# A sixth weight slot, three projections moved into tile 1's recurrence, and V gathers traded against U gathers beside the recurrence

## What is computed

```python
mix = concatenate([att, hgrn_output(o, hg, hg_norm_gain)])
x = x + einsum('btm,md->btd', mix, w_out)                  # 1024 x 1024 weights
h2 = rms_norm(x, norm2_gain)
# peer_ffn, per token: 8 heads x 16 chosen experts = 128 rows of U and 128 rows of V
q = (h2 @ w_query).reshape(T, 8, 2, 128)                   # 1024 x 2048 weights
s = einsum('thcd,hcnd->thcn', q, sub_keys)
...                                                        # two top-16, then top-16 of the 256 sums: eidx, gate
act = gelu(einsum('thkd,td->thk', expert_u[eidx], h2))     # one dot per row of U
y = einsum('thk,thkd->td', gate * act, expert_v[eidx])     # weighted sum of rows of V
```

## Time and profile before

| | us |
|---|---|
| three runs, median (lowest to highest) | 2190.84 (2189.47 to 2190.89) |
| the profiled execution | 2188.74 |
| its span in the trace | 2186.6 |

### The profile page before, as it was taken

One profiled execution on the slowest core, in us unless ns is written; L12 is line 12 of the kernel. 1 busy time (PEld: TensorE's weight loads), 2 busy tenths in 40 slices (PEclk: granted clock), 3 DMA queues, 4 the chain that ended last, 5 costly groups with the idle time before them and its releaser, 6 DMA issues.

```text
span 2186.6 us, 15704 instructions
## 1 busy us (share of the span) xinstructions
PE 1222.7 (56%) x4932; PEld 548.7 (25%) x4932; DVE 1261.9 (58%) x2795; ACT 372.6 (17%) x1034; POOL 1166.5 (53%) x1197
## 2 busy tenths in 40 slices
PE   5898777555864436744553675466467322223553
PEld 2544343234321333311123331123323000000110
DVE  3344331866595997765439786544977656565001
ACT  1221211121121111311111131111113100001211
POOL 3012110232477754577774457777445767777773
PEclk9798889776998567866656786666578656555787
DMA  9211183556899989999998999999899999999997
GB/s 331 99 59 59 58 297 119 186 201 221 331 410 409 409 331 397 378 377 409 409 409 328 397 390 376 409 409 409 305 397 352 374 409 409 409 410 409 411 409 294
DMA packets 204306, 722.04 MB, mean 330 GB/s; under 512 B 23248, under 2 KB 25536, under 8 KB 203072
## 3 DMA queue, kind: packets, MB, share of 16 engines
q0 software_dynamic: 171168, 624.01, 73.5%
q1 hardware_dynamic: 33056, 97.03, 12.2%
HBM read 704.71 MB, written 15.70 MB: 329 GB/s over the span
## 4 chain that ended last, share of the span: by engine, by line
DMA 26%; PE 24%; DVE 16%; POOL 13%; issue 5%; ACT 4%; DVEq 0%; POOLq 0%; ACTq 0%
DMA arena<-peer_expert_v,idx_v 16%; POOL arena L595 8%; DMA arena<-peer_expert_u,idx_all 7%; DVE arena L1384 7%; PE PD L1041 5%; POOL arena L589 4%; PE PB L1251 4%; PE PD L963 3%; PE PB L1230 2%; PE PA L1181 2%; PE PA L1230 2%; DMA lev<-w_out 2%; DMA lev<-peer_w_query 2%; DVE w L1521 2%; PE PA L1041 1%
## 5 line engine op out<-in xcount | busy, mean ns | idle before, releaser
L589 POOL DMA_INDIRECT arena<-peer_expert_u,idx_all x576 | 542.5, 942 | 507.7 <-DVE arena L1384 259.6
L1384 DVE SCALAR_TENSOR_TENSOR arena<-arena,PC 128x1024 f32<-128x1024 f32 x576 | 677.1, 1217 | 142.8 <-DMA arena<-peer_expert_u,idx_all 135.6
L595 POOL DMA_INDIRECT arena<-peer_expert_v,idx_v x576 | 567.3, 985 | 228.7 <-issue 143.1
L1041 PE MATMUL PD<-arena,diag_v 128*32 128x512 f32 x1792 | 365.6, 897 | 497.6 <-DMA arena<-peer_expert_v,idx_v 436.5
L1041 PEld LDWEIGHTS PD<-arena,diag_v 128*32 128x32 f32 x1792 | 80.0, 141 | 749.8 <-issue 749.8
L817 ACT ACTIVATE diag_v<-consts,gate_all 128x32 f32<-128x32 f32 x576 | 136.7, 309 | 535.0 <-PE PD L1041 410.7
L963 PE MATMUL PD<-arena 128*128 128x512 f32 x384 | 174.6, 610 | 0.0
L1449 DVE TENSOR_TENSOR PA<-PA,consts 128x128 f32<-128x128 f32 (+4 forms) x56 | 14.0, 250 | 219.9 <-PE PA L1099 219.6
L1041 PE MATMUL PA<-arena,diag_v 128*32 128x512 f32 x512 | 85.5, 800 | 80.3 <-DMA arena<-peer_expert_v,idx_v 80.3
L963 PEld LDWEIGHTS PD<-arena 128*128 128x128 f32 x384 | 73.4, 196 | 85.9 <-issue 85.3
L1230 PE MATMUL PB<-lev,rows_t 128*128 128x512 f32 x160 | 83.0, 672 | 11.0 <-ACT rows_t L922 5.6
(11 more groups left out here) (271 smaller groups left out, 1527.4 us busy)
## 6 DMA issues: line engine op xcount, KB each, us to landing
lev<-w_out SPq DMA_DIRECT2D x40, 512.0 KB, 8.1
lev<-peer_w_query SPq DMA_DIRECT2D x40, 512.0 KB, 8.1
arena<-w_in SPq DMA_DIRECT2D x8, 2048.0 KB, 14.3
arena<-peer_expert_u,idx_all POOLq DMA_INDIRECT x576, 11.2
arena<-peer_expert_v,idx_v POOLq DMA_INDIRECT x576, 11.4
arena<-w_in POOLq DMA_DIRECT2D x4, 2048.0 KB, 8.8
act<-staged SPq DMA_DIRECT2D x4, 1796.0 KB
staged<-arena POOLq DMA_DIRECT2D x5, 1024.0 KB, 5.5
```

The lines of the kernel that those rows point to most:

```text
L589: pool.indirect_dma_start(slot, None, peer_expert_u[0], bass.IndirectOffsetOnAxis(ap=idx_all[:, k:k + 1], axis=0)).then_inc(arrived, 16)
L595: pool.indirect_dma_start(slot, None, peer_expert_v[0], bass.IndirectOffsetOnAxis(ap=idx_v[:, k:k + 1], axis=0)).then_inc(arrived, 16)
L1041: ins = pe.matmul(psum[c * STRIP:(c + 1) * STRIP, half * 512:(half + 1) * 512], diag_v[:, at * STRIP:(at + 1) * STRIP], ring[slot_of[v_pla ...
L1384: eng.scalar_tensor_tensor(out=slot, in0=slot, scalar=1.0, in1=h2_dots[:, :], op0=ALU.mult, op1=ALU.mult, accum_out=out).then_inc(free, 1)
```

## The change

`WO_RING` becomes 6. The sixth slot is the first 1024 columns of `act`; the sub keys move to its last 2048 columns. SyncE's first six loads wait in addition for the tile's attention to be done, and in tile 0 for the stores of tile 0's keys and values. In tile 1 the last six items go to head1, head3, head5, twice "levels" and "gram2" in place of head0 to head5. Dots move from the recurrence (27 to 19 per tile) and the last place (26 to 25) to the attention heads (63 to 72); of the 19 V groups that are left over, nine stay with the heads and ten go beside the recurrence.

```diff
-WO_RING = 5
+WO_RING = 6
...
-DOT_PLACES = [("start", 7)] + [(f"head{h}", 7) for h in range(HEADS)] + [
-    ("subtract", 3), ("levels", 5), ("multiply", 3), ("masks", 4)] + [(f"gram{h}", 3) for h in range(HG)] + [
-    ("out", 12), ("rows", 26)]
-LEFT_PLACES = [("start", 2)] + [(f"head{h}", 2) for h in range(HEADS)] + [
-    ("levels", 1)]
+DOT_PLACES = [("start", 8)] + [(f"head{h}", 8) for h in range(HEADS)] + [
+    ("subtract", 2), ("levels", 4), ("multiply", 2), ("masks", 3)] + [(f"gram{h}", 2) for h in range(HG)] + [
+    ("out", 12), ("rows", 25)]
+LEFT_PLACES = [("start", 1)] + [(f"head{h}", 1) for h in range(HEADS)] + [
+    ("levels", 3), ("masks", 3), ("gram1", 2), ("gram2", 2)]
...
-    ("levels", 2), ("masks", 1), ("gram1", 1), ("gram2", 1)]] + [(1, f"head{h}", 1) for h in range(6)]
+    ("levels", 2), ("masks", 1), ("gram1", 1), ("gram2", 1)]] + [
+    (1, f"head{h}", 1) for h in (1, 3, 5)] + [(1, "levels", 2), (1, "gram2", 1)]
...
-        keys_t = act[:, 0:2 * PH * NKEY]
+        keys_t = act[:, ST_W - 2 * PH * NKEY:ST_W]
...
-        w_out_sb = lev[:, :].rearrange("p (r n) -> p r n", r=WO_RING)
+
+        w_out_ring = [lev[:, n * D:(n + 1) * D] for n in range(WO_RING - 1)] + [act[:, 0:D]]
...
-                    sp.dma_start(w_out_sb[:, slot, :], src[c % DC * P:(c % DC + 1) * P, :]).then_inc(wo_in[slot], 16)
+                    sp.dma_start(w_out_ring[slot], src[c % DC * P:(c % DC + 1) * P, :]).then_inc(wo_in[slot], 16)
...
                 sp.wait_ge(ho_done, HG * (t + 1))
+                if t == 0:
+                    sp.wait_ge(first_stored, 16 * 6)
+                sp.wait_ge(att_done, heads_before(t + 1) // HEADS)
                 for c in range(WO_RING):
                     load_w_out(c)
...
-                if t == 0:
-                    sp.wait_ge(first_stored, 16 * 6)
                 sp.dma_start(keys_t, sub_keys_t).then_inc(keys_in, 16)
```

More of the change, by code:

```diff
@@ L1230, in streamed @@
                         last = pe.matmul(out[:, half * 512:(half + 1) * 512], rows_t[:, c % DC * P:c % DC * P + n],
-                                         w_out_sb[:, slot, half * 512:(half + 1) * 512],
+                                         w_out_ring[slot][:, half * 512:(half + 1) * 512],
                                          start=(c % DC == 0), stop=(c % DC == DC - 1))
```

## The result

The changed kernel takes 2178.01 us (median of 6 runs, 2176.30 to 2180.53), the kernel before 2193.09 us beside it (6 runs, 2189.47 to 2198.98). The ratio is 0.9929, with a 95% interval of 0.9914 to 0.9944: **faster by 0.7%, some 15.6 us**, where 34 us were forecast. The direction is right and the time lies in the range; less than half of the size came. The profiled execution took 2176.3 us around a span of 2174.1 us, so the two spans differ by 12.5 us.

What follows compares the result with a forecast made beforehand. From about 585 us the kernel was taken as bound by bytes at the DMA ceiling of 409 to 411 GB/s. Terms -25 - 7 + 1 - 3 = -34 us took 2190.84 to 2157 us, range 2142 to 2184.

Steps and rivals of the forecast that it cites:

- main term: Tiles 3 and 4: dots exchanged for V groups fill the DMA engines' holes in the recurrences, -25 us.
- second rival: Half comes back: last dots hold up the search, -25 becomes -12 and -7 becomes -3, near 2174 us; chance 0.20.
- The exchange: Tiles 3 and 4: more gathers in the recurrence, fewer in the heads; nine tenths of 27.6 us loss goes, -25 us.
- The sixth slot: Projections from mix to search: last chunks' loads asked for earlier, 4.4 us per tile; -7 us for tiles 3 and 4.
- Tile 2: Only dots move: recurrence 4.6 us shorter, 5.6 us more lost, projections give 4.4 back; +1 us (bounds -4 to +7).
- Tile 1: Mix 7 us later, search 2 to 3 us later, V gathers sooner worth 6.4 us; -3 us (bounds -6 to +4).
- (b): Tile 1's recurrence: two items at "levels", copied by ScalarE before the exponential, make it later, +5.9 us.
- (c): Tile 1's recurrence: the item in front of the last gram adds up to 7 us, taken as +4.5 us.
- (a): Tile 1's heads get shorter with three items in place of six, -3 us (bounds -6 to +2).
- The gain from V gathers that go sooner: Tile 1: V gathers start some 8 us sooner, about five more are there when the search starts, 6.4 us.
- The V groups did not hold up the recurrence: First rival, tiles 3 and 4: V groups lengthen the recurrence, mix at 117 us, about 2208 us; chance 0.09.
- Gathers were not slowed beside it: Third rival: gathers beside VectorE in the recurrences take 2.50 us, +45 us per tile, near 2280 us; chance 0.02.

Runs made afterwards that it cites:

- Run 5: Run 4 with the four dots of "levels" moved in front of the recurrence's first subtraction: 2163.56 us, ratio 0.9864 to the kernel before.
- run 3: The kernel before with only the exchange of dots for V groups; five slots, items as before: 2178.35 us, ratio 0.9938.
- run 1: The kernel before with only the sixth slot, moved keys and SyncE's waits; dots, V groups and items as before: 2183.3 us, ratio 0.9962.
- run 4: The change with the six items of tile 1 left in its heads: 2168.08 us, ratio 0.9895 to the kernel before.
- run 6: Run 4 with SyncE's load of the sub-keys put behind the last w_out chunk: 2161.08 us, ratio 0.9864 to the kernel before.
- run 7: Run 4 with eight places for w_out chunks, two more in columns of `act`, sub-keys loaded behind them: 2157.26 us, ratio 0.9833 to the kernel before.
- run 2: The kernel before with only the change's places for tile 1's items: 2194.36 us, ratio 1.0011.
- Run 12: Run 4 with tile 1's dots where the kernel before had them: 2172.97 us, ratio 0.9914 to the kernel before.

## Why the prediction came out too large

**What bounds the kernel** was read rightly: from tile 1's search on, the gains and losses above are stretches in which the DMA engines left or regained the ceiling of 409 GB/s. Direction and mechanism of the main term hold, and so does its schedule. The heads of tile 3, from the first matmul of attention to the first of the recurrence, became 177.9 - 146.6 = 31 us shorter (34.6 forecast; the DMA engines had no loss in them). From the recurrence's first matmul, the V groups at "masks" end after 43.5 us, the last gram starts after 72.4 and the mix is there after 88.3 (43, 73 and 90 forecast). That the time lies in the range is owed to the range's reach over the second rival, not to the sum: three of its four terms are off.

**The exchange, -25 us: measured -16.2** (27.6 us of losses became 11.4, shown by the stretches). The step that failed is "with about 5 of them already there when the recurrence starts", after which the prediction sees nothing that could hold up a gather. GpSimd has issued 17 by then, all buffers are taken, and VectorE's next dot comes 7.5 us after the recurrence's first matmul. I had looked at what arrives and not at what frees a buffer, although the prediction itself reads such a wait, 3.46 us, in the kernel before. Run 5, with four dots in front, brings the loss at the starts to nothing. Without the sixth slot (run 3) the starts lose 5.4 us in place of 11.1; no run shows why.

**The sixth slot, -7 us beside tiles 3 and 4's searches: measured -1.5** (7.0 + 12.4 became 8.4 + 9.5). Alone the slot makes these two tiles 4.9 us shorter, beside the exchange not at all (runs 1 and 4). What failed is that I priced it with the queue of before, in which the gathers had thinned out by the mix, and added it to an exchange that fills that very queue. The prediction lists "six weight chunks of 512 KB" as work that keeps the DMA engines busy at the mix, and does not ask when the last chunks of that same stream, behind the megabyte of sub-keys, land. Runs 6 and 7 show it: with the chunks in place the searches of tiles 3 and 4 get 5.6 and 9.7 us back. That the slot by itself gives 8.3 us, near the forecast's 7, is in part luck: 5.7 of it are in tile 1, where the forecast put none. The sentence that the 15 us stall ahead of the search "mostly goes" was wrong too: 15.69 us are in the trace, and run 7, with 13.30, shows that the stall need not cost anything. The second rival, half of it coming back because the last stage's chain holds up the search, is nearest to what happened.

**Tile 2, +1 us: measured -2.4**, within its bounds, but not by the forecast's parts. The recurrence became 5.3 us shorter (4.6 forecast) and loses 1.0 us more, not 5.6; the search loses 2.6 less. Alone, the exchange costs tile 2 4.4 us of losses, and the slot gives that back and more.

**Tile 1, -3 us: measured +4.6**, past the bound of +4. (b) was right: the exponential is 6.6 us later (5.9 forecast), and with (c) the recurrence is 9.9 us longer, 10.4 forecast. (a) was wrong: the recurrence starts 61.3 us behind tile 0's expert numbers, 61.7 before. Moving the items shortens the heads by 7.4 us alone (run 2), but here they also got nine dots more, and the items themselves take longer than the 7.03 us counted (9.71, 7.03 and 8.73 us, and 14.78 and 7.49 where they went: 47.7 us in all for 8.21 + 5 x 7.03 = 43.4). The gain from V gathers that go sooner, 6.4 us, does not show in tile 1 either: they fill the 17 buffers before the search (the stall of 13.10 us), after which GpSimd has no lead for the gathers of 2 to 2.5 us beside the search, and 10 us are lost there. In the kernel before the same slow gathers stand beside that search, and the rate stays at 406 GB/s and more. Run 12 leaves open whether the sooner gathers are worth anything to tiles 1 and 2 together.

**The rivals.** The V groups did not hold up the recurrence: it is 88 us long, under the 100 from which that would decide. Gathers were not slowed beside it either: the slowest of tile 3's takes 1.30 us and of tile 4's 1.46, against 2.49 beside tile 1's search. The Trainium skill, page "GPSIMD Engine Reference", section "Key points", has GpSimd contend with VectorE's instructions of two SBUF inputs: the trace agrees with it for the search's wide operations, and hardly for the recurrence's products.

## What to carry to other kernels

When a change fills an idle stretch of a shared queue, price again every transfer that used to pass through it in the quiet: here weight chunks that landed in 7.8 us took 16.1, and the chain behind them gave back part of what was won. A prefetch ring's stall is read from both ends: what the next buffer waits for (a consumer that is busy elsewhere for 7 us) counts as much as how many transfers are asked for. And of two parts that are worth 8 and 14 us alone, a third that costs 2 alone can cost 7 beside them, so measure the parts one by one in the changed kernel, by leaving one out.

## What the runs showed of the hardware

The items in tile 1's heads: with one in each of six heads TensorE is busy for 52.5 of 60 us and the mean granted clock there is 0.93; with one in every second head it is busy for 35.5 of 57 us and the clock is 0.77, a mean of stretches at 2.4 and at 1.2 GHz. Within the items themselves the clock is 1.00 where they take 7.03 us, 0.80 in the one of 8.73 and 0.72 in the one of 9.71, and length times clock is 7.0 us each time. Ahead of the one of 9.71 TensorE had stood still for 9.5 us, and the clock in the 10 us before it is 0.50. So part of what was saved by taking work off TensorE, 4.4 us in three items, went into the clock. The rows:

```profile
414.00:474.00 60.00, 52.52 (x155) 25.54 (x153) 46.00 (x93) 9.86 (x38) 33.87 (x37) 0.93 0.95 339
```
```profile
415.00:472.00 57.00, 35.46 (x106) 18.29 (x106) 46.97 (x95) 8.13 (x35) 33.97 (x37) 0.77 0.95 348
```

The first is of the change without the items' move (4), the second of the change.

Loads that SyncE issues share the DMA engines with the gathers, and get half of them while both have work. For tile 3's mix in the change (1203 to 1214 us) the view of DMA issues gives packets, MB and share of the engines' time, of GpSimd's queue (q0) and of SyncE's (q1):

```profile
q0 software_dynamic: 612, 2.25, 51.6%
q1 hardware_dynamic: 609, 2.23, 50.6%
```

In the kernel before, around its mix (1213 to 1226 us), SyncE's queue moved 3.17 MB and GpSimd's 1.97, since fewer gathers were left. That is a large part of why a chunk took 7.8 us there and takes 16.1 now. The time from issue to landing also holds what stands ahead in the same queue. Ahead of tile 3's mix the change asks for six chunks within 2.3 us (from 1196.28), and the sixth, issued at 1198.55, lands 20.3 us later:

```profile
act<-w_out SPq DMA_DIRECT2D x1, 512.0 KB, 20.3
```

So six chunks, 3.15 MB, took 22.6 us, 139 GB/s, a third of the 409 and not half. But SyncE's queue moved 4.08 MB in these 22.6 us: another 512 KB were asked for just ahead of the six, at 1195.51, and 1.5 MB (with the sub-keys) from 1205.24 on. And none of its packets show before 1198.5 us. The Trainium skill, page "DMA: Bandwidth & Descriptors", section "Queues, rings and completion order", says that each DMA engine takes turns between the queues that have work, a packet at a time. The trace agrees with it: 612 and 609 packets in the 11 us above.
